# Issuing an MLP's DMA transposes from ScalarE behind the copy that feeds them, instead of from SyncE between loads

## What is computed

```python
def sq_relu_mlp(hn, w1, w2):
    return jnp.square(jax.nn.relu(hn @ w1)) @ w2

h = h + sq_relu_mlp(rmsnorm(h, ln_mlp[i]), mlp_w1[i], mlp_w2[i])
```

## Time and profile before

| | before |
|---|---|
| median of 3 runs | 2525.71 us (2525.06 to 2526.45) |
| the profiled execution | 2525.19 us |
| its span, first to last instruction | 2523.5 us |
| PE busy | 2515.6 us (100%) |
| DVE busy | 1827.6 us (72%) |
| ACT busy | 1488.9 us (59%) |
| DMA, mean rate | 210 GB/s |
| DMA transposes from SP at L509 | 96, of which 64 in the quarters |

### The profile page before, as it was taken

The page is one execution under the profiler, slowest core; times in us unless marked ns, Lnnn a source line. Parts: engine busy times, 40 slices in busy tenths (PEclk is TensorE's granted clock), DMA queues, the critical chain, the costliest instruction groups (busy, mean ns, idle before and its releaser), DMA issues.

```text
span 2523.5 us, 29875 instructions
## 1 busy us (share of the span) xinstructions
PE 2515.6 (100%) x11496; PEld 2086.8 (83%) x11496; DVE 1827.6 (72%) x2046; ACT 1488.9 (59%) x1814; POOL 103.2 (4%) x208
## 2 busy tenths in 40 slices
PE   9999999999999999999999999999999999999999
PEld 8888888888888888888888888888888888888887
DVE  6778787878768668668577667767686785775765
ACT  6755556655565465564556667655654645546653
POOL 2010000000000000000001002100000000000000
PEclk9999999999999999999999999999999999999999
DMA  8877888887686776766767764458867667677873
GB/s 279 239 238 242 236 246 239 232 230 219 196 212 192 228 197 205 217 187 229 213 204 227 217 185 142 141 159 211 206 204 221 186 225 214 183 226 201 230 219 131
DMA packets 344815, 530.29 MB, mean 210 GB/s; under 512 B 131664, under 2 KB 137032, under 8 KB 344672
## 3 DMA queue, kind: packets, MB, share of 16 engines
q1 hardware_dynamic: 340496, 518.16, 70.1%
q0 software_dynamic: 2656, 8.58, 1.4%
q10 hardware_dynamic: 1520, 1.64, 0.2%
HBM read 486.38 MB, written 2.16 MB: 194 GB/s over the span
## 4 chain that ended last, share of the span: by engine, by line
PE 100%; DMA 0%; DVE 0%; ACT 0%; ACTq 0%; issue 0%
PE acc_a L2199 9%; PE acc_a L2201 9%; PE acc_a L2200 9%; PE acc_b L2199 9%; PE acc_b L2201 9%; PE acc_b L2200 9%; PE mid L2199 3%; PE mid L2200 3%; PE mid L2201 3%; PE tp L2200 2%; PE tp L2201 2%; PE tp L2199 2%; PE acc_a L2214 2%; PE acc_b L2214 2%; PE mid L2216 2%; PE mid L2215 2%
## 5 line engine op out<-in xcount | busy, mean ns | idle before, releaser
L1400 DVE TENSOR_TENSOR w<-raw,w 128x1024 fp32r<-128x1024 f32 (+1 forms) x816 | 986.2, 1218 | 472.1 <-ACT w L742 467.6
L742 ACT ACTIVATE w<-raw 128x1024 fp32r<-128x1024 f32 (+1 forms) x844 | 883.2, 1053 | 675.4 <-PE acc_b L2201 216.0
L2199 PE MATMUL acc_a<-w,xa 128*128 128x512 f32 x760 | 298.4, 393 | 0.0
L2201 PE MATMUL acc_a<-w,xa 128*128 128x512 f32 x760 | 296.1, 390 | 0.0
L2200 PE MATMUL acc_a<-w,xa 128*128 128x512 f32 x760 | 295.7, 389 | 0.0
L2199 PE MATMUL acc_b<-w,xa 128*128 128x512 f32 (+1 forms) x736 | 285.6, 388 | 0.0
L2201 PE MATMUL acc_b<-w,xa 128*128 128x512 f32 (+1 forms) x736 | 283.1, 385 | 0.0
L2200 PE MATMUL acc_b<-w,xa 128*128 128x512 f32 (+1 forms) x736 | 282.9, 384 | 0.0
L2201 PEld LDWEIGHTS acc_a<-w,xa 128*128 128x128 f32 x760 | 142.7, 188 | 30.0
L2200 PEld LDWEIGHTS acc_a<-w,xa 128*128 128x128 f32 x760 | 142.8, 188 | 28.7
L2199 PEld LDWEIGHTS acc_a<-w,xa 128*128 128x128 f32 x760 | 142.8, 188 | 28.7
(11 more groups left out here) (417 smaller groups left out, 4674.5 us busy)
## 6 DMA issues: line engine op xcount, KB each, us to landing
raw<-in_mlp_w SPq DMA_DIRECT2D x512, 512.0 KB, 4.5
raw<-in_ssm_in_w SPq DMA_DIRECT2D x161, 512.0 KB, 5.9
raw<-in_ssm_out_w SPq DMA_DIRECT2D x64, 512.0 KB, 5.3
raw<-in_ple_gate_w SPq DMA_DIRECT2D x64, 512.0 KB, 4.1
raw<-in_mla_out_w SPq DMA_DIRECT2D x32, 512.0 KB, 3.9
scratch<-cumulative POOLq DMA_DIRECT2D x16, 512.0 KB, 7.0
rows<-in_ssm_conv_w SPq DMA_DIRECT2D x32, 256.0 KB, 6.4
raw<-in_ple_proj_w SPq DMA_DIRECT2D x8, 512.0 KB, 4.5
```

Of the source, the lines that this page charges most:

```text
L742: act.activation(w_hi[:, g % SPL, :, 0:cols], raw[:, g % RAW, :, 0:cols], ACT.Copy)\
L1400: dve.tensor_tensor(w_lo[:, g % SPL, :, 0:cols], raw[:, g % RAW, :, 0:cols], w_hi[:, g % SPL, :, 0:cols].bitcast(F32), ALU.subtract).then_ ...
L2199: pe.matmul(dst, xh, wh, start=first and k == 0, stop=False)
L2201: mm = pe.matmul(dst, xl, wh, start=False, stop=last and k == 1)
```

## The change

SP no longer issues the four turns of each quarter. ScalarE issues them itself, directly behind the plane copy in `unzip`: it waits for its own copies (semaphore `wd`) and issues the two transposes. Buffers, semaphores, the joins and their places stay. SP steps its count of copies over the sixteen of a layer, so that its remaining turns wait for the right ones.

```diff
@@ block.sync, mlp(layer) @@
+                w.skip("wd", 4 * 4)
                 for q in range(4):
                     if q:
                         unit(up, c512(q * D + 512))
-                        unit(up, c512(q * D + 2 * 512), jobs={3: [turn_block]})
-                        unit(up, c512(q * D + 3 * 512), jobs={3: [turn_block]})
+                        unit(up, c512(q * D + 2 * 512))
+                        unit(up, c512(q * D + 3 * 512))
                     else:
                         unit(up, c512(2 * 512))
-                        unit(up, c512(3 * 512), jobs={1: [turn_block], 3: [turn_block]})
-                    rows_of_pair(down, 0, q * KT, {3: [turn_block], 11: [turn_block]})
+                        unit(up, c512(3 * 512))
+                    rows_of_pair(down, 0, q * KT)
@@ block.scalar @@
+            def turn_block(n):
+                words, turned = words_of_two[n % 2], turned_of_two[n % 2]
+                act.wait_ge(S["wd"], n + 1)
+                for t in range(NT):
+                    act.dma_start_transpose(turned[:, :, :, t * P:t * P + P].rearrange("p s f n -> p (s f) n"),
+                                            words[:, t].rearrange("p s n -> p (s n)")).then_inc(s_turned[n % 2], 16)
@@ block.scalar, mlp, unzip @@
                         last.then_inc(S["wd"], 1)
+                        turn_block(n)
```

## The result

| | before | after |
|---|---|---|
| median | 2525.39 us (2524.53 to 2527.14, 6 runs) | 2534.88 us (2530.84 to 2538.26, 6 runs) |
| the profiled execution | 2525.19 us | 2535.48 us |
| its span | 2523.5 us | 2533.7 us |

The changed kernel is slower: the ratio of the times is 1.0034, 95% interval 1.0024 to 1.0044. That is 9.5 us, outside the predicted range of 2524.3 to 2530.5. The first rival, with 0.09, had said 2533.7.

The account below looks back on a forecast made before the run. PE was taken as the bound, busy 2515.6 of 2523.5 us. All terms summed to 0 against the profiled run, so the forecast was the median, 2525.7 us, with a range of 2524.3 to 2530.5.

Parts of the forecast that it names:

- The first rival: On ScalarE a turn is as long as on SP, about 5.0 to 5.2 us; costs 8 us, 2533.7; chance 0.09.
- Step 1: On SP's queue, losing 32 turns lets loads go up to 5.0 us sooner, worth nothing.
- Step 2: Behind each plane copy ScalarE gets its own wait and two transposes, in all 32 x 2.7 = 86 us of ScalarE.
- C: ScalarE's time from the end of the copies to the next split, taken as 2.7 us, range 1.3 to 5.2.
- rows 4 to 6: Trace rows of SP's turns: 5.04 us right behind a load, ending as it lands; 2.60 us with no fresh load.
- rows 10: Trace rows of two plain ScalarE DMAs during SP's turn: 1.16 us together, read as queues not holding each other.
- Step 3, the places: Splits queued behind turns: no PE wait up to 5.6 us at ordinary pieces, 3.5 in first quarters, 4.9 in pair units.
- The close turns: Each layer's first quarter, two copies two pieces apart: no wait up to C = 3.5, beyond it 2(C - 3.5).
- the working: Sum for PE's wait: 2(C - 3.5) in each layer's first quarter; in pair units each us beyond C = 4.9.
- Step 3, the price of a hole: A gap with PE idle in a first quarter, priced 2(C - 3.5); 6.4 us for two layers at C of 5.1.
- Step 4: Transposes land 3 to 5.6 us after issue; the fourth turn's join allows 9 us, so the cost is nothing.
- The rival of PE's small waits: In the pair units, sooner loads or joins end PE's idle time, at most 7 us, giving 2518.7; chance 0.02.

Follow-up runs that it names:

- m1_turns: A separate kernel of turns and loads alone, ten settings three times each; second transpose 1.36 to 1.37 us quiet, 1.69 to 2.19 with one SP load.
- e1_late: The changed kernel, but the first two turns of each layer's first quarter stay on SP; 2527.61 us against 2525.25 before (1.0008).
- e8_load_after: The changed kernel, but SP keeps back the load just ahead of a turn until ScalarE has issued the turn; 2525.48 us (0.9999).

## Why the prediction was wrong

**Step 1, SP's freed time: right.** It was worth nothing, as taken. e4_held, in which SP keeps its turns and ScalarE only loses its time, is as slow as the change.

**Step 2, the cost of a turn on ScalarE: this is the step that failed.** C was taken as 2.7 us, and measured 5.0 in the median, 4.0 to 5.85 over the 32 turns. Its small parts were right: 0.03 us of own wait and 0.10 us of return. The term of the transposes was not, and the fault is in the reading of rows 4 to 6. They show that a turn ends when the load ahead of it lands. They don't show whether it waits for that load as one on its queue or as one in the DMA engines, since in the trace of before every turn and every load go by SP. I closed the gap with rows 10, where two plain DMAs of ScalarE went through during SP's turn, and took from this that queues don't hold each other. But plain DMAs aren't held by a load either (0.33 to 0.45 us in m1_turns). The row was about another operation, and had nothing to say about a transpose. With the range of C stated up to 5.2 and the two readings undecided by any row, the rival should have had something near half of the chance and not 0.09, and the range of the time, which stopped at C = 4.7, should have reached the rival's 2533.7.

**The rule weighed there.** The Trainium skill (Perfetto Trace Analysis, section DMA Instruction — HWDGE (DVE, Sync)) has a shared generator that one sequencer locks. It pointed the right way, to a turn on ScalarE that waits for SP's load. But a load is issued in 0.33 to 0.47 us and the turn is held until about when it lands, 3.5 to 6.4 us after issue, so these runs show a wait that goes with the transfer and not with its issue.

**Step 3, the places: right.** No wait at ordinary pieces up to C = 5.6: none in the changed kernel at 4.0 to 5.3, and 0.39 us in e1_late at 5.92. The close turns of the first quarter: with 4.62 and 5.00 the working gives 4.62 + 5.00 - 7.0 = 2.6 us, and PE was idle for 2.47. The pair units: a price from C = 4.9 on was right, but "each us is paid" was too much. With the C measured there (six of 5.33 to 5.85, two under 4.9) the working gives 4.4 us; the weight loads waited 4.1 us longer, and the time grew by about 2 (2.0 in the profile of the change, 2.4 in e1_late).

**Step 3, the price of a hole: too small.** It was set at the idle time alone. Three of the four holes in the two profiles of the changed kernel brought a stretch at half the clock, and cost 1.8 to 1.9 us more than their idle time (4.36 less 2.47, 3.83 less 1.95, 5.07 less 3.23), some 0.3 of which is also lost where the clock stays. In the profile shown first, the 10.2 us are 4.4 of idle time in the holes (2.47 and 1.95), 0.6 of slow start behind them, 3.2 of slow clock, and 2.0 elsewhere, mostly in the pair units. That the rival's 2533.7 came so near is in part luck: its C of 5.1 was too high for the first quarters, where it had 6.4 us for the holes and their idle time was 4.4, and the clock, which it did not have, more than made up for that.

**Step 4, the landing: right in its price.** The join never waits for a DMA in the first profile of the changed kernel. In the second it does once, for 1.89 us at 1816.5, behind a turn whose transposes landed 8.9 and 9.6 us after issue, later than the 7.5 that the forecast had as the slowest so far; PE has no idle time there. **The rival of PE's small waits: right in what it named, wrong in how they go.** They do go, for 5.2 us of its bound of 7, but only if the turn lands early and the join is moved as well. The change did neither.

## What to carry to other kernels

The second of two DMA transposes holds the sequencer that issues it until about when the load issued just ahead has landed, be that load on the same queue or on the other one (shown for SP and ScalarE). So a turn isn't made cheaper by another issuer, but by issuing it before the load and not behind it. Before giving it to an engine that feeds the bound engine, add up all such holds that fall within the bound engine's lead: one of 4.7 us cost nothing here, a pair of 4.6 and 5.0 cost 4.4 us. And where every row has two things together (here turn and load on one queue), they can't say which of the two is the cause; the chances should stay near even until a row parts them.

## What the runs showed of the hardware

- A first transpose of this size takes 1.24 to 1.34 us of the sequencer in m1_turns, one behind another 1.34 to 1.37 when no load is in flight, up to four in a row. With one load of 512 KB in flight the second takes 1.7 to 2.2 us there and 2.6 to 4.4 in the changed kernel, and it ends shortly before the load lands.
- A transpose lands 2.9 us after its issue with no load just ahead of its turn and 6.0 us behind one (medians of e8_load_after and of after); in the quiet setting of m1_turns it is 3.2 to 3.4.
- Idle gaps of PE of 1.95, 2.22, 2.41, 2.47, 2.54 and 3.23 us, between stretches of dense matmuls, were followed by about 3.4 us at a granted clock of 0.50; gaps of 1.64 and 2.23 us were not. The length of the gap alone doesn't tell which.
